# Mixer A's attention loop: turn and sum one pair later, a ring of five, gates inside the weighing, lower tile weighed on GpSimd, copies between exps

## The reference, cut to what matters

```
proj = h @ w_in                      # q, three pairs of k and v, gate logits
gates = sigmoid(gl + b_gate)         # (token, head, branch)
for branch in (selected, window):
    s = q @ k.T * dh**-0.5 + rel_bias[t5_bucket(dist)]
    p = softmax(where(causal, s, -1e30))
    o += gates[..., branch] * (p @ v)
o += gates[..., 0] * o_cmp           # the compressed branch
x = x + o @ w_out
```

## Time and profile before

| | us |
|---|---|
| runs (3): lowest, median, highest | 1318.6, 1318.75, 1319.12 |
| span of the profiled execution | 1316.2 |
| median of the runs less the span | 2.55 |
| PE busy in the span | 1283.2 |
| DVE busy | 815.2 |
| ACT busy | 652.0 |
| POOL busy | 259.4 |

### The profile page before, as it was taken

The page is one execution under the profiler, slowest core; times in us unless marked ns, Lnnn a source line. Parts: engine busy times, 40 slices in busy tenths (PEclk is TensorE's granted clock), DMA queues, the critical chain, the costliest instruction groups (busy, mean ns, idle before and its releaser), DMA issues. The chain is left out here.

```text
span 1316.2 us, 19228 instructions
## 1 busy us (share of the span) xinstructions
PE 1283.2 (97%) x7247; PEld 1074.7 (82%) x7247; DVE 815.2 (62%) x1214; ACT 652.0 (50%) x955; POOL 259.4 (20%) x339
## 2 busy tenths in 40 slices
PE   6999999999999999999999999999999999999997
PEld 5986788888799988888888788888877778888886
DVE  3468665555564486655555855556789867755554
ACT  4338654444443376543444654445444684544442
POOL 5320110000000021102000489701176120200000
PEclk9999999999999999999999999999999999999999
DMA  9971556555456653567755565654544336565551
GB/s 291 263 133 22 167 178 191 185 180 186 155 192 192 161 133 89 161 210 167 235 190 171 181 192 181 217 192 143 192 129 142 130 113 210 189 192 190 183 188 44
DMA packets 155658, 225.80 MB, mean 172 GB/s; under 512 B 13027, under 2 KB 107467, under 8 KB 155596
## 3 DMA queue, kind: packets, MB, share of 16 engines
q1 hardware_dynamic: 141008, 208.36, 50.8%
q0 software_dynamic: 9840, 11.60, 4.4%
q10 hardware_dynamic: 4748, 5.01, 1.2%
HBM read 223.59 MB, written 1.27 MB: 171 GB/s over the span
## 5 line engine op out<-in xcount | busy, mean ns | idle before, releaser
L597 DVE TENSOR_TENSOR units_lo<-raw_units,units_hi 128x2048 fp32r<-128x2048 f32 x96 | 222.2, 2314 | 154.1 <-ACT units_hi L551 154.1
L197 PE MATMUL bank<-units_hi,turned_hi 128*128 128x512 f32 (+1 forms) x792 | 307.3, 388 | 3.0 <-DVE units_lo L180 1.3
L180 DVE TENSOR_TENSOR units_lo<-raw_units,units_hi 128x2048 fp32r<-128x2048 f32 (+2 forms) x103 | 233.1, 2271 | 113.7 <-ACT units_hi L172 113.5
L199 PE MATMUL bank<-units_hi,turned_lo 128*128 128x512 f32 (+1 forms) x792 | 302.3, 382 | 0.0
L198 PE MATMUL bank<-units_lo,turned_hi 128*128 128x512 f32 (+1 forms) x792 | 302.0, 381 | 0.0
L172 ACT ACTIVATE units_hi<-raw_units 128x2048 fp32r<-128x2048 f32 (+2 forms) x103 | 193.2, 1886 | 119.5 <-PE bank L199 86.9
L551 ACT ACTIVATE units_hi<-raw_units 128x2048 fp32r<-128x2048 f32 x96 | 183.5, 1911 | 103.4 <-PE bank L199 95.5
L197 PE MATMUL bank<-units_hi,second_hi 128*128 128x512 f32 (+1 forms) x560 | 218.7, 390 | 0.4 <-ACT rows L2311 0.4
L199 PE MATMUL bank<-units_hi,second_lo 128*128 128x512 f32 (+1 forms) x560 | 216.5, 387 | 0.0
L198 PE MATMUL bank<-units_lo,second_hi 128*128 128x512 f32 (+1 forms) x560 | 216.4, 386 | 0.0
L197 PEld LDWEIGHTS bank<-units_hi,turned_hi 128*128 128x128 f32 x792 | 149.4, 189 | 32.7 <-DVE units_lo L180 3.0
(11 more groups left out here) (351 smaller groups left out, 1818.1 us busy)
## 6 DMA issues: line engine op xcount, KB each, us to landing
raw_units<-in_ffn_w_up SPq DMA_DIRECT2D x88, 512.0 KB, 4.8
raw_units<-in_ffn_w_in SPq DMA_DIRECT2D x88, 512.0 KB, 4.6
raw_units<-in_ffn_w_down SPq DMA_DIRECT2D x22, 1024.0 KB, 5.0
raw_units<-in_ffn_w_out SPq DMA_DIRECT2D x22, 1024.0 KB, 5.0
raw_units<-in_w_in SPq DMA_DIRECT2D x18, 1024.0 KB, 5.1
raw_units<-in_b_w_q SPq DMA_DIRECT2D x12, 1024.0 KB, 5.1
raw_units<-in_a_w_in SPq DMA_DIRECT2D x10, 1024.0 KB, 11.3
raw_units<-in_kv_w SPq DMA_DIRECT2D x6, 1024.0 KB, 5.2
```

What stands on the lines that cost most here:

```text
L180: dve.tensor_tensor(lo, raw, hi.bitcast(F32), ALU.subtract).then_inc(m.lo_done, 1)
L197: pe.matmul(out, lh, rh, start=start, stop=False, skip_group_check=True)
L199: return pe.matmul(out, ll, rh, start=False, stop=True, skip_group_check=True)
L597: dve.tensor_tensor(m.WL[:, slot(n0 + j), :], m.RAW[:, slot(n0 + j), :], m.WH[:, slot(n0 + j), :].bitcast(F32), ALU.subtract).then_inc(m.l ...
```

## The change

Four things are changed in this loop. Turn and sum move one step later (3 and 4 in place of 2 and 3), and the ring of weights has five pairs in place of three; the step of out_hi and out_lo follows. DVE no longer multiplies the reciprocals with the gates; a weighing takes the reciprocal and the gate as two column operands. DVE weighs only the upper token tile (128x256) of each head, and the lower one (128x128) is weighed on POOL, in a loop of its own ahead of its wait for the last biasing; the turn waits for both. ACT copies the turned weights of a head right behind that head's two exps, where it copied both heads behind all four.

```diff
--- before.py
+++ after.py
@@ -1336,8 +1336,8 @@
     return T, T // 4, T % 4, br
 
 
-RING_PAIRS = 3
-TURN_AFTER, SUM_AFTER = 2, 3
+RING_PAIRS = 5
+TURN_AFTER, SUM_AFTER = 3, 4
 HALVES_A = ((0, S, 1), (S, S + P, 0))
 
 
@@ -1366,7 +1366,8 @@
         if TURN_AFTER <= p < NPA + TURN_AFTER:
             i = p - TURN_AFTER
             for par in range(2):
-                pe.wait_ge(m.s("a_weighted"), 4 * i + 2 * par + 2)
+                pe.wait_ge(m.s("a_weighted"), 2 * i + par + 1)
+                pe.wait_ge(m.s("a_low_weighted"), 2 * i + par + 1)
                 if i >= 1:
                     pe.wait_ge(m.s("a_turned_copied"), 2 * (i - 1) + par + 1)
                 w = m.A.PB[:, i % RING_PAIRS, par, :]
@@ -1415,20 +1416,35 @@
                                      accum_out=m.A.NM[:, p, par, tok:tok + 1]).then_inc(m.s("a_biased"), 1)
 
 
+def gate_column_a(m, i, par, tok):
+
+    T, G, r, br = pair_a(i)
+    at = 3 * (4 * (2 * G + par) + r) + 1 + br
+    return m.A.GATE[:, tok, at:at + 1]
+
+
 def weigh_pair_a_vector(dve, m, i):
-    T, G, r, br = pair_a(i)
+
     dve.wait_ge(m.s("a_exp"), 4 * (i + 1))
     dve.reciprocal(m.A.RD[:, i, :, :], m.A.RS[:, i, :, :]).then_inc(m.s("a_factor"), 1)
-    dve.wait_ge(m.s("a_factor"), 2 * i + 1)
-    first = 8 * G + r
-    g = m.A.GATE.rearrange("p t (h b) -> p h t b", b=3)[:, first:first + 5:4, :, 1 + br]
-    dve.tensor_tensor(m.A.RD[:, i, :, :], m.A.RD[:, i, :, :], g, ALU.mult).then_inc(m.s("a_factor"), 1)
-    dve.wait_ge(m.s("a_factor"), 2 * i + 2)
+    dve.wait_ge(m.s("a_factor"), i + 1)
+    a, b, tok = HALVES_A[0]
     for par in range(2):
-        for a, b, tok in HALVES_A:
+        w = m.A.PB[:, i % RING_PAIRS, par, a:b]
+        dve.tensor_scalar(w, w, m.A.RD[:, i, par, tok:tok + 1], gate_column_a(m, i, par, tok), ALU.mult, ALU.mult)\
+            .then_inc(m.s("a_weighted"), 1)
+
+
+def weigh_low_a_gpsimd(pool, m):
+
+    pool.wait_ge(m.s("gate_steps"), 4)
+    a, b, tok = HALVES_A[1]
+    for i in range(NPA):
+        pool.wait_ge(m.s("a_factor"), i + 1)
+        for par in range(2):
             w = m.A.PB[:, i % RING_PAIRS, par, a:b]
-            dve.tensor_scalar(w, w, m.A.RD[:, i, par, tok:tok + 1], None, ALU.mult)\
-                .then_inc(m.s("a_weighted"), 1)
+            pool.tensor_scalar(w, w, m.A.RD[:, i, par, tok:tok + 1], gate_column_a(m, i, par, tok), ALU.mult,
+                               ALU.mult).then_inc(m.s("a_low_weighted"), 1)
 
 
 def attend_a_vector(dve, m):
@@ -1438,7 +1454,7 @@
         if 2 < p < NPA + 1:
             weigh_pair_a_vector(dve, m, p - 1)
         for T in range(7):
-            if LAST_PAIR[T] + 4 == p:
+            if LAST_PAIR[T] + SUM_AFTER + 1 == p:
                 out_lo(dve, m, "a", T, T, m.pb[6 + T % 2][:, 0:S])
     out_lo(dve, m, "a", 7, 7, m.pb[7][:, 0:S])
 
@@ -1458,11 +1474,15 @@
 
 def exp_pair_a_scalar(act, m, p):
     for par in range(2):
-        for x, (a, b, tok) in enumerate(HALVES_A):
-            act.wait_ge(m.s("a_biased"), 4 * p + 2 * par + x + 1)
-            w = m.A.PB[:, p % RING_PAIRS, par, a:b]
-            act.activation(w, w, ACT.Exp, bias=m.A.NM[:, p, par, tok:tok + 1], scale=-1.0,
-                           accum_out=m.A.RS[:, p, par, tok:tok + 1]).then_inc(m.s("a_exp"), 1)
+        exp_head_a_scalar(act, m, p, par)
+
+
+def exp_head_a_scalar(act, m, p, par):
+    for x, (a, b, tok) in enumerate(HALVES_A):
+        act.wait_ge(m.s("a_biased"), 4 * p + 2 * par + x + 1)
+        w = m.A.PB[:, p % RING_PAIRS, par, a:b]
+        act.activation(w, w, ACT.Exp, bias=m.A.NM[:, p, par, tok:tok + 1], scale=-1.0,
+                       accum_out=m.A.RS[:, p, par, tok:tok + 1]).then_inc(m.s("a_exp"), 1)
 
 
 def attend_a_scalar(act, m):
@@ -1472,13 +1492,13 @@
 
     for p in range(2, NPA + SUM_AFTER):
         for T in range(7):
-            if LAST_PAIR[T] + 4 == p:
+            if LAST_PAIR[T] + SUM_AFTER + 1 == p:
                 out_hi(T)
-        if p < NPA:
-            exp_pair_a_scalar(act, m, p)
-        if TURN_AFTER <= p < NPA + TURN_AFTER:
-            i = p - TURN_AFTER
-            for par in range(2):
+        for par in range(2):
+            if p < NPA:
+                exp_head_a_scalar(act, m, p, par)
+            if TURN_AFTER <= p < NPA + TURN_AFTER:
+                i = p - TURN_AFTER
                 act.wait_ge(m.s("a_turned"), 2 * i + par + 1)
                 if i >= 2:
                     act.wait_ge(m.s("a_summed"), 2 * (i - 1))
@@ -3443,6 +3463,7 @@
             tables_gpsimd(pool, m)
             bias_a_gpsimd(pool, m, range(0, 10))
             compress_gpsimd(pool, m)
+            weigh_low_a_gpsimd(pool, m)
             pool.wait_ge(m.s("a_biased"), 4 * NPA)
             bias_b_gpsimd(pool, m, range(RINGB))
             tile_scales_gpsimd(pool, m, 0, 0.5)
```

## The result

The changed kernel took 1323.57 us in the median of 10 runs (1320.95 to 1325.61) against 1318.48 of before in 10 runs; the ratio is 1.0033, 95% interval 1.0020 to 1.0046. Twelve more runs, measured later on chip 7, gave 1323.59 against 1318.03 (1.0039, 1.0024 to 1.0054). The means differ by 4.3 us (1323.17 and 1318.87) and by 5.2 us (1324.12 and 1318.90). The forecast was 1320.0 with a range of 1317.3 to 1321.9 and 0.81 on "within 0.2%": it missed, and on the slow side.

What follows compares the result with a forecast made beforehand. PE, busy 97%, was taken as the limit, waiting in mixer A's loop on a ring ended by ACT's copy. Steady state unchanged, head and tail 1.2 us later: 1318.75 + 1.2 = 1320.0, range 1317.3 to 1321.9.

Steps and rivals of the forecast that it cites:

- The steady state: Mixer A's attention loop once filled: biasing, exps, copy, turn, sums and score form a ring, 6.01 us before, 6.00 after.
- Double steps: Two pairs of mixer A's attention loop, one round of the ring of waits; forecast at 6.00 us.
- the copy between the exps: ACT's first copy comes 0.89 us earlier, the second stays last; costed at nothing in the steady state.
- The weighing was off the path: At PE's turn, DVE's weighing ends 0.17 us before the copy and is not the limit.
- rival 1: DVE's weighing, not the copy, ends PE's wait, so PE runs freed: 2.3 us earlier, 1316.5; chance 0.15.
- Head and tail: Loop's ends: last exps start 1.0 us earlier, 2.2 us more work follows them; output projection 1.2 us later.
- rival 3: TensorE's clock falls after the head's stall, 1.7 us lost on top of 1.2: 1321.7; chance 0.04.
- the longer pipeline: Turn and sum a pair later add a step at head and tail; forecast net 1.2 us later.
- Rivals 2 and 4: In the weighing: DVE and POOL lock each other out, 1323.3, chance 0.09; POOL late by itself, 1325, chance 0.02.

Runs made afterwards that it cites:

- e2: Kernel before with only ACT's order changed to two exps, copy, two exps, copy; 1320.88 us, ratio 1.0016.
- e3: Kernel before with only the weighing changed (gates as second column operand, lower tile on GpSimd); ratio 1.0035, measured again with 12 runs 1.0006.
- e4: Changed kernel, but in the step that copies pair 0 ACT copies each head ahead of its exps; ratio 1.0048, again with 12 runs 1.0021.
- a2: The changed kernel measured once more, nothing edited, against before; 12 runs, 1323.59 us, ratio 1.0039.
- e1: Kernel before with only turn and sum a pair later and the ring of five; 1322.55 us, ratio 1.0042.
- g1: Kernel before with only pair 0's copies put behind pair 3's exps, a stall alone; 1326.18 us, ratio 1.0066.
- f3: Whole change, but with ACT's order copy, two exps, copy, two exps in every step; against before 1318.55 us, ratio 1.0006.

## Why the prediction was wrong

**The steady state was right.** Double steps of 6.00 were forecast, 6.01 measured; the copy between the exps changed places with a half-turn and was worth 0.00 (e2). The weighing was off the path (e3), as the 0.17 us in the earlier trace rows said against the waits' row that names it: rival 1 is out.

**Head and tail at full clock were right.** The second half of turn 1 was forecast 5.94 us after pair 2's score (105.41 - 99.47); it came 5.93 after (103.54 - 97.61). From the last exps to the output projection 9.19 us were forecast (147.69 - 138.50) and 9.02 measured (148.56 - 139.54). e4, the changed kernel without the long stall, has a loop of 47.52 us where about 47.7 were expected. Behind the loop the two kernels differ by 0.4 us, where nothing was forecast.

**The step that failed is rival 3, the clock.** The forecast moved pair 0's copies behind pair 3's exps and put PE's stall there at about 2 us, but then took as evidence that the clock had stayed at 1.00 after 1.22 us of idle time, and gave the fall 0.04, so the sum held the clock at nothing. A stall of 1.2 us says nothing of one twice as long. In all four profiles with more than 2 us of idle time at turn 1 (changed, a2, e1, g1) the clock fell; in the other ten, with 1.3 us or less, it fell once (f3). Its price of 1.7 us was taken from one stretch. The loop of 48.22 us (147.69 - 99.47) that this working gives at full clock sets the measured prices: 1.4 us in e1, 50.95 - 48.22 = 2.7 in the changed kernel's first profile, 3.0 in a2 for its two falls together, and in g1 4.3. So 1.7 was a fair price for a short fall, and nothing in the forecast allowed for a longer or a second one. With 2.7 the rival's sum is 1.2 + 2.7 = 3.9 us, against a loop 4.06 us longer and mean times 4.3 and 5.2 us longer.

In a2's measurement the mean times differ by 5.2 us and the mean clocks by .0031, an estimated 4.1 us; 1.1 are left for the longer pipeline, forecast at 1.2. Of the 4.1 us the loop of a2's profile accounts for 3.0. What the change has to do with the other 1.1 stays open. Half clock comes elsewhere too, in some executions and not in others: before had 0.51 from 17 to 20 us and half clock again at 85 us, e1 0.57 from 362 to 366 us.

**Rivals 2 and 4.** DVE's weighing with two columns took 418 ns in the median, and POOL's 534. The 348 that I took for DVE's is the median of a row that mixes 128x256 and 128x128; the 128x256 alone took 365 ns in the mean in the loop before. Still, two of each a pair are far from the 0.73 us each and 1.4 us each from which they would have decided. POOL's go from 436 to 740 ns where one alone took 383. The Trainium skill's rule on the shared port (SBUF — State Buffer, Who interferes with whom), by which one engine waits out a whole instruction of the other, fits the spread on POOL's side: the longest is 0.36 us above the nearest undisturbed one, less than one DVE weighing (0.42). On DVE's side the longest weighing was 473 ns against 411 for the shortest, so none shows a wait for a whole POOL one. Both had slack, and it changed nothing.

## What to carry to other kernels

Where engines hand work round a ring, add up the ring over as many steps as it spans, and ask of each moved instruction whether the last link still stands where it stood: here both heads' copies had to leave the place behind the exps, not one. A deeper pipeline costs a step at head and tail, and while it fills it can leave TensorE idle for long enough that its clock falls; price such a stall as the stall plus the half clock behind it. Compare the length of the touched stage between profiles before the times of whole runs, since what differs ahead of the stage from execution to execution (the loop began at 97.5 to 103.3 us) is as large as the effect sought, and medians of 4 or 5 runs did not average it out.

## What the runs showed of the hardware

TensorE's granted clock fell to 0.50 after idle time of 2.2 to 3.0 us at turn 1 in four of four profiles and stayed there for 3.4 to 10.2 us. With 0.57 and 0.74 us of idle time in two pieces it stayed at 1.00 twice (e4) and fell once (f3); with 0.40 and 0.73 us in two pieces at the tail it stayed three times (changed, e4 twice) and fell once (a2). So for two such short pieces the same stream gave either outcome, and the runs do not show what decides it.

The two levels seen are those that the Trainium skill names (TensorE: Matmul & The Clock Gate, Part 1): full and half, nothing between them in any window without a change. The times of one kernel spread with the clock: those of before on one chip go from 1316.01 us at a mean clock of .999 to 1325.14 at .994.
